# Expert stage of a two-layer hybrid decoder: output step and scatter of the first expert pair moved into the third pair

## The reference

```python
xn = rms_norm(x, norm_g)
g_w, g_idx = top_k(softmax(xn @ w_rg + b_rg), 1)            # 1 of 4 groups
e_w, e_idx = top_k(softmax(e_logits of that group), 2)      # 2 of its 8 experts
combine = ...                                               # 256 x 32 weights, 2 nonzero a row
hid = silu(xn @ w1[e]) * (xn @ w3[e])                       # w1, w3: 1024 x 256, each e of 32
y   = (hid * combine[:, e]) @ w2[e]                         # w2: 256 x 1024
return x + sum over e of y
```

## Time and profile before

| what | value |
|---|---|
| median of 3 runs | 1045.63 us (1043.52 to 1047.7) |
| the profiled execution's own time | 1050.6 us |
| its span | 1048.5 us |
| busy in the span: PE, PEld, DVE, ACT, POOL | 969.1, 782.0, 480.3, 469.0, 21.9 us |
| moved by DMA | 293.37 MB, 280 GB/s over the span |
| mean granted clock of TensorE | 0.968 of full |

### The profile page before, as it was taken

One profiled execution on the slowest core, in us unless ns is written; L12 is line 12 of the kernel. 1 busy time (PEld: TensorE's weight loads), 2 busy tenths in 40 slices (PEclk: granted clock), 3 DMA queues, 4 the chain that ended last, 5 costly groups with the idle time before them and its releaser, 6 DMA issues. The chain is left out here.

```text
span 1048.5 us, 19318 instructions
## 1 busy us (share of the span) xinstructions
PE 969.1 (92%) x7942; PEld 782.0 (75%) x7942; DVE 480.3 (46%) x809; ACT 469.0 (45%) x723; POOL 21.9 (2%) x39
## 2 busy tenths in 40 slices
PE   5999999999999999979779999999999899998784
PEld 5998899899886666544478988998998766665342
DVE  5446775567753222111353567655586622221112
ACT  6455555565543333311354555565654443332111
POOL 1010100000000000000000101000000000000000
PEclk9999999999999999988889999999999999999886
DMA  8744544556888999999855245535669799999993
GB/s 283 229 136 161 161 167 161 202 181 227 325 351 322 412 421 420 419 420 421 337 162 190 97 161 167 190 133 202 242 227 363 284 375 422 420 419 419 421 420 124
DMA packets 85480, 293.37 MB, mean 280 GB/s; under 512 B 16976, under 2 KB 17040, under 8 KB 60816
## 3 DMA queue, kind: packets, MB, share of 16 engines
q1 hardware_dynamic: 85392, 292.12, 73.1%
HBM read 291.05 MB, written 1.05 MB: 279 GB/s over the span
## 5 line engine op out<-in xcount | busy, mean ns | idle before, releaser
L1153 ACT ACTIVATE w_high<-weight_ring 128x1024 fp32r<-128x1024 f32 x168 | 176.7, 1059 | 209.7 <-PE ps_a L723 151.0
L1432 DVE TENSOR_TENSOR w_low<-weight_ring,w_high 128x1024 fp32r<-128x1024 f32 x168 | 202.9, 1226 | 140.1 <-ACT w_high L1153 139.5
L721 PE MATMUL ps_a<-xnT_high,w_high 128*128 128x256 f32 x704 | 202.8, 288 | 4.0 <-DVE xnT_low L1438 4.0
L723 PE MATMUL ps_a<-xnT_high,w_low 128*128 128x256 f32 x704 | 200.5, 285 | 0.0
L722 PE MATMUL ps_a<-xnT_low,w_high 128*128 128x256 f32 x704 | 199.9, 284 | 0.0
L721 PEld LDWEIGHTS ps_a<-xnT_high,w_high 128*128 128x128 f32 x704 | 134.5, 191 | 6.6 <-DVE xnT_low L1438 4.8
L722 PEld LDWEIGHTS ps_a<-xnT_low,w_high 128*128 128x128 f32 x704 | 134.8, 191 | 0.5 <-issue 0.5
L723 PEld LDWEIGHTS ps_a<-xnT_high,w_low 128*128 128x128 f32 x704 | 133.8, 190 | 0.0
L1805 DVE TENSOR_TENSOR y_lo<-ps_b,y_hi 128x512 fp32r<-128x512 f32 x64 | 44.3, 692 | 151.8 <-ACT y_hi L1402 149.9
L1121 PEld LDWEIGHTS ps_b<-fold,h 128*128 128x128 f32 x512 | 70.6, 204 | 34.7 <-issue 29.8
L1363 ACT ACTIVATE h<-ps_b 128x512 f32<-128x512 f32 x64 | 38.3, 598 | 128.0 <-PE ps_b L1044 128.0
(11 more groups left out here) (334 smaller groups left out, 1560.7 us busy)
## 6 DMA issues: line engine op xcount, KB each, us to landing
weight_ring<-in_w_in_dram SPq DMA_DIRECT2D x64, 1024.0 KB, 5.2
units_over_splits<-in_w_dram SPq DMA_DIRECT2D x60, 1024.0 KB, 24.0
units_over_attention<-in_w_dram SPq DMA_DIRECT2D x46, 1024.0 KB, 15.9
weight_ring<-in_w_dram SPq DMA_DIRECT2D x40, 1024.0 KB, 21.4
units_over_branches<-in_w_dram SPq DMA_DIRECT2D x30, 1024.0 KB, 18.6
weight_ring<-in_w_branch_dram SPq DMA_DIRECT2D x12, 1024.0 KB, 5.3
unit_over_gates<-in_w_dram SPq DMA_DIRECT2D x10, 1024.0 KB, 18.6
weight_ring<-in_w_out_dram SPq DMA_DIRECT2D x8, 1024.0 KB, 6.6
```

Source lines behind the costliest of these rows:

```text
L721: mm(dst, wh, xh, start=row == 0 and s % 2 == 0, stop=False, skip_group_check=True)
L723: last = mm(dst, wl, xh, start=False, stop=row == rows - 1, skip_group_check=True)
L1153: A(mix_buf(whi, i), mix_raw(i), ACT.Copy).then_inc(hi_ready, 1)
L1432: v.tensor_tensor(mix_buf(wlo, i), mix_raw(i), mix_buf(whi, i).bitcast(F32), ALU.subtract).then_inc(lo_ready, 1)
```

## The change

The output step and the scatter of pair 0 leave the second pair. The third pair now does both, right after its first gather, and then, after its second hidden step and ahead of its second gather, the output step of pair 1. From the fourth pair on the order is as before. The numbering of the units changes with it: 4 to 9 are now w1 and w3 of the experts 2, 3 and 4, 10 and 11 are w2 of pair 0, 12 and 13 are w1 and w3 of expert 5, and 14 and 15 are w2 of pair 1. From 16 on it is as before. The once-places over y, XT1 and selectT now hold the units 9, 5 and 7.

```diff
-ONCE_UNITS = (4, 5, 9)
+ONCE_UNITS = (9, 5, 7)
...
             gather()
-            if not last:
+
+            if p == 2:
+                outputs(0)
+                steps.append(("scatter", 0))
+            elif 2 < p and not last:
                 outputs(p - 1)
         hidden_T(2 * p)
         if p:
             select_next()
         hidden(2 * p + 1)
-        if last:
+        if last or p == 2:
             outputs(p - 1)
...
         if p:
             gather()
-            if not last:
+            if 1 < p and not last:
                 steps.append(("scatter", p - 1))
         hidden_T(2 * p + 1)
```

## The result

| | before | changed |
|---|---|---|
| median | 1046.39 us (1043.52 to 1047.7, 4 runs) | 1056.51 us (1056.19 to 1056.73, 4 runs) |
| profiled execution, its span | 1050.6, 1048.5 us | 1056.73, 1054.7 us |

The ratio is 1.0095, with a 95% interval of 1.0072 to 1.0118. The change makes the kernel 10 us slower where 4.8 us were forecast, and the time lies 1.0 us above the range. The same pair measured again in another job gave 1.0077 (1.0047 to 1.0108).

The account below looks back on a forecast made before the run. Weight transfers bound the expert stage, through the time the DMA queue runs dry before its plateau. Idle grows from 2.7 to 5.1 us a layer, 2 x 2.4 = 4.8 us, giving 1050.4 us; range 1044.5 to 1055.5.

Parts of the forecast that it names:

- The end of the stage is set by the transfers, dry time is never made good: Expert stage: DMA queue idle before the plateau delays the end, 2.7 us a layer before; TensorE's own later delay is recovered.
- Stalls of 1.0, 1.5 and 0.7 us: TensorE waits at hT of experts 2 and 3 and at scatter 0, summing to 3.2 us a layer.
- Releases at 8.0, 13.2, 18.7, 22.6, 22.9 us: SP's issues after the fourth, counted from the stage's first; before they stood at 12.0, 12.3, 14.0, 20.2, 21.0.
- 2.4 us a layer: Extra idle time of the DMA queue in each expert stage, 5.1 us after the change against 2.7 before.
- The chain: Model of the unit stream: each starts 1.7 us after issue or at the previous end, and takes 2.5 us.
- 2.0 us of smaller gaps: Ahead of the plateau: shortfall inferred from a landing at 353.5 where the model had 350.8; used for the upper bound.
- the one on hidden step 4: Third pair: hidden 4 starts at 332.88 + 1.06 = 333.94, its gather at 335.81, output 0 at 336.93.
- rival B: Clock drops after the 1.5 us stall at hT of expert 3; 3 us more idle a layer, 1056.4; chance 8%.
- The sum: Both layers together: 2 x 2.4 = 4.8 us, moving the median from 1045.63 to 1050.4.
- Rival A: Early release of unit 4 closes the gap from 328.1 to 330.1, gaining 2.0 us a layer, 1041.6; chance 14%.
- TensorE's waits in the last third unchanged: Sign that the forecast is right: TensorE's waits late in the expert stage stay as before.

Follow-up runs that it names:

- b_delay: Kernel before with 26 idle matmuls ahead of hidden step 4, order and places of units unchanged; median 1054.81 us, ratio 1.0079 to before.
- a_fill_short: Changed kernel with 4 and 5 idle matmuls in the waits ahead of the hT steps of experts 2 and 3; 1048.98 us, 1.0014 to before.
- a_once457: Changed kernel with units 4, 5 and 7 in the once-places instead of 9, 5 and 7; median 1057.63 us, ratio 1.0099 to before.
- a_tail_fill: Changed kernel with 12, 12 and 9 idle matmuls in the waits for w2 of pairs 12, 13, 14; 1053.70 us, 1.0063 to before.
- the pair with filled tails: Kernel before and changed kernel, both with idle matmuls in the w2 waits of pairs 12, 13, 14; 1045.25 and 1053.70 us.
- a_late_gather: Changed kernel with the gathers starting in the third pair; median 1047.29 us, ratio 0.9996 to before.
- c_late_gather: Kernel before with gathers starting in the third pair and once-places of units 5 and 9 swapped; median 1044.54 us, ratio 0.9983 to before.
- b_again: Kernel before, unchanged, run again for a second trace; median 1048.68 us, ratio 1.0024 to before.

## Why the prediction was wrong

The direction and the bound held, and so did the mechanism of stalls, late releases and a dry queue. The mechanism lacked a term: the lower clock that the stalls bring on.

- *The end of the stage is set by the transfers, dry time is never made good.* Shown by b_delay: 5.6 us more lost for a TensorE 5.7 us late with nothing else changed, and the last landing 5.0 us later. From the first issue to the last expert unit's landing, the four layers of before took 197.2, 194.8, 194.8 and 195.6 us, mean 195.6, and the four of the changed kernel 198.9, 199.4, 198.9 and 198.6, mean 198.95. That is 3.35 us a layer, where the dry time says 3.8.
- *Stalls of 1.0, 1.5 and 0.7 us.* Measured 1.02, 1.45, 0.82.
- *Releases at 8.0, 13.2, 18.7, 22.6, 22.9 us.* Right in a_fill_short to 0.1 us, where the clock is kept up. In the changed kernel the last three came at 19.7, 24.3 and 24.7.
- *2.4 us a layer.* 2.1 in a_fill_short. The chain itself was good: its 2.7 and 5.1 us of idle time, each with 1.7 for the stream's start, make 4.4 and 6.8, and 4.55 (before) and 6.65 (a_fill_short) were lost. The "2.0 us of smaller gaps" that it was thought to be short by are not in the bytes.
- **The step that failed** is the one on hidden step 4, taken at its length of before, 1.86 us, and with it rival B at 8%. I put B aside because "1.5 is below 2.49", the idle time ahead of the drop at 442. One idle time that was followed by a drop is no lower bound for those that are. Here 1.02 and 1.45 us stood 5.5 us apart, and the clock fell every time: in both layers of both traces of the changed kernel, of a_once457 and of a_tail_fill, 8 of 8. B's price was also wrong: 3 us were reckoned from 6.8 us at the lower level, but the clock came back after hidden step 4, and it cost 1.7.
- *The sum.* 2 x (2.1 + 1.7) = 7.6 us where 4.8 stood. The measured values are 8.1 (1.0077), 8.45 (the pair with filled tails) and 10. The half to two and a half microseconds between them and 7.6 are no more than the medians of the kernel before differ by from job to job (3.3).
- *Rival A* (the early release wins): unit 4's release is real and worth 1.2 us a layer, or 2.0 by the landings (a_once457). That the stalls outweighed it follows from the chain and from the five releases, which a_fill_short had at the forecast times. That the changed order without stalls would be level with before (2.6 against 2.7 us idle) was not measured: a_late_gather is level, but it also took the gathers out of the second pair, and still had waits of 0.79 and 0.82 us.
- *TensorE's waits in the last third unchanged*, and so no loss there: the tails were not unchanged, but they vary as much within the kernel before.

## What to carry to other kernels

Where a ring of buffers feeds a stage that the transfers bound, the cost of a reordering is read from the release times up to the point where the queue stays full, and from nothing behind it. GB/s over that stretch measured it here to about half a microsecond, where medians of the unchanged kernel lay up to 3.3 us apart. A step that is moved away may have been the cover of someone else's copy: look at what stands between a bank's writer and its next user afterwards. Price an idle time on TensorE twice, once as itself and once as the matmuls behind it at the lower clock. And give an experiment that takes the suspected waits away a partner that differs in nothing else: a_late_gather beside the kernel before seemed to clear the moved output step, and beside c_late_gather it does not.

## What was unexpected of the hardware

- The granted clock fell to 0.50 behind idle times of 1.02 and 1.45 us with work between them. It did not fall behind waits of 0.79, 0.79 and 0.82 us in a_late_gather. Yet late in b_again's second layer (1016 to 1018 us) it fell behind waits of 0.80 and 0.97 us, 3.1 us apart, with one of 1.13 us some 7 us earlier. No single length of idle time parts these cases.
- The order of landings can slip without any loss of bandwidth. In the trace of before two neighbouring issues took 18.0 and 20.5 us to land:

```profile
362.91 0.43 SPq L550 DMA_DIRECT2D units_over_branches<-in_w_dram  x1
...
364.60 0.33 SPq L550 DMA_DIRECT2D units_over_branches<-in_w_dram  x1
```

```profile
364.60:385.10 20.50, 20.50 (x215) 13.79 (x208) 4.69 (x15) 7.74 (x18) 0.00 (x0) 1.00 1.01 420
```

Their landings are 4.2 us apart where a unit takes 2.5 at this rate, and yet 420 GB/s were moved. One part of a transfer being late would look like this; that was not tried, and neither was whether such slips make up the rest of the scatter from run to run.
